# Block 1's recurrence in compact 64x64 tiles for all head pairs at once, its preparation inside the mixer's input product, attention scores from 64-row operands

## What is computed

```python
    for l in range(DEPTH):
        h = rms_norm(x, norm_ffn1[l])
        x = x + 0.5 * swiglu(h, ffn1_gate[l], ffn1_up[l], ffn1_down[l])
        h = rms_norm(x, norm_mix[l])
        p = h @ w_in[l]
...
    a = jax.nn.sigmoid(a0.astype(f32) + a_lo @ a2.astype(f32))
    g = jax.nn.sigmoid(g_lo) @ g2.astype(f32)
    kk = (k * k_k.astype(f32)).reshape(B, S, H, N)
    kk = kk / jnp.maximum(jnp.sqrt(jnp.sum(kk * kk, axis=-1, keepdims=True)), 1e-12)
...
    def step(state, inp):
        r_t, w_t, k_t, v_t, kk_t, b_t = inp
        sa = jnp.einsum('bhvk,bhk->bhv', state, -kk_t)
        state = (state * w_t[:, :, None, :] + sa[..., None] * b_t[:, :, None, :]
                 + v_t[..., None] * k_t[:, :, None, :])
        return state, jnp.einsum('bhvk,bhk->bhv', state, r_t)
```

## Time and profile before

| | |
|---|---|
| median of 3 runs | 3650.39 us (3649.76 to 3652.47) |
| the profiled execution | 3649.7 us, span 3647.9 us |
| instructions in the profile | 35779 |
| mean granted TensorE clock | 0.897 of full |

### The profile page before, as it was taken

One profiled execution on the slowest core, in us unless ns is written; L12 is line 12 of the kernel. 1 busy time (PEld: TensorE's weight loads), 2 busy tenths in 40 slices (PEclk: granted clock), 3 DMA queues, 4 the chain that ended last, 5 costly groups with the idle time before them and its releaser, 6 DMA issues. The chain is left out here.

```text
span 3647.9 us, 35779 instructions
## 1 busy us (share of the span) xinstructions
PE 3145.8 (86%) x14332; PEld 2549.1 (70%) x14332; DVE 1496.5 (41%) x1969; ACT 986.8 (27%) x1336; POOL 1204.2 (33%) x574
## 2 busy tenths in 40 slices
PE   8999978888699999999999998996534678999677
PEld 6888857778578888777887887884432556897346
DVE  4333435554443344745253221834676243000543
ACT  3222221110232232454233332112220142222131
POOL 3444432211134444553444443442000033444312
PEclk9999987777699999999999999997765689999878
DMA  3332210000023332222233233231210223332002
GB/s 129 97 102 96 87 61 1 1 0 1 1 87 96 93 105 92 81 81 81 93 98 93 93 98 109 88 98 47 15 21 19 41 85 96 93 93 93 0 18 75
DMA packets 91444, 251.28 MB, mean 69 GB/s; under 512 B 33440, under 2 KB 34592, under 8 KB 90400
## 3 DMA queue, kind: packets, MB, share of 16 engines
q1 hardware_dynamic: 82080, 247.09, 22.2%
q10 hardware_dynamic: 9216, 2.10, 0.3%
HBM read 240.51 MB, written 6.29 MB: 68 GB/s over the span
## 5 line engine op out<-in xcount | busy, mean ns | idle before, releaser
L436 POOL TENSOR_TENSOR weight_ring_r<-weight_ring,weight_hi_r 128x1024 fp32r<-128x1024 f32 (+2 forms) x412 | 1032.3, 2506 | 1641.6 <-ACT weight_hi_r L429 1641.6
L429 ACT ACTIVATE weight_hi_r<-weight_ring 128x1024 fp32r<-128x1024 f32 (+2 forms) x412 | 448.5, 1089 | 1637.1 <-PE acc L636 1275.1
L634 PE MATMUL acc<-p_r,weight_hi_r 128*128 128x512 f32 x1680 | 665.4, 396 | 19.1 <-POOL weight_ring_r L436 12.6
L636 PE MATMUL acc<-p_r,weight_ring_r 128*128 128x512 f32 x1680 | 659.6, 393 | 0.0
L635 PE MATMUL acc<-scr_r,weight_hi_r 128*128 128x512 f32 x1120 | 440.2, 393 | 0.0
L634 PEld LDWEIGHTS acc<-p_r,weight_hi_r 128*128 128x128 f32 x1680 | 316.4, 188 | 89.9 <-POOL weight_ring_r L436 19.4
L636 PEld LDWEIGHTS acc<-p_r,weight_ring_r 128*128 128x128 f32 x1680 | 316.3, 188 | 73.9
L635 PE MATMUL acc<-p_r,weight_hi_r 128*128 128x512 f32 x888 | 346.7, 390 | 0.0
L634 PE MATMUL acc<-scr_r,weight_hi_r 128*128 128x512 f32 x768 | 310.1, 404 | 15.6 <-DVE p_r L655 10.7
L636 PE MATMUL acc<-scr_r,weight_ring_r 128*128 128x512 f32 x768 | 304.9, 397 | 0.0
L635 PE MATMUL acc<-h_r,weight_hi_r 128*128 128x512 f32 x696 | 276.2, 397 | 0.0
(11 more groups left out here) (567 smaller groups left out, 4910.4 us busy)
## 6 DMA issues: line engine op xcount, KB each, us to landing
weight_ring<-in_weights SPq DMA_DIRECT2D x372, 512.0 KB, 3.5
weight_ring<-in_weights SPq DMA_DIRECT2D x32, 704.0 KB, 4.0
weight_ring<-in_weights SPq DMA_DIRECT2D x8, 640.0 KB, 3.9
x<-in_x SPq DMA_DIRECT2D x4, 512.0 KB, 6.9
lift<-h SPq DMA_DIRECT2D x1, 2048.0 KB, 8.8
p<-lift SPq DMA_DIRECT2D x8, 256.0 KB, 10.7
p<-lift SPq DMA_DIRECT2D x1, 2048.0 KB, 8.8
out<-x SPq DMA_DIRECT2D x1, 2048.0 KB, 6.3
```

Source lines behind the costliest of these rows:

```text
L429: self.nc.scalar.activation(self.r.weight_hi[:, ahead, 0:width], self.weight_ring[:, r, 0:width], ACT.Copy)\
L436: self.nc.gpsimd.tensor_tensor(rest, raw, hi, ALU.subtract).then_inc(self.weights_split, 1)
L634: pe.matmul(out, hi, op.hi(kx), start=kx == 0, stop=False)
L636: mm = pe.matmul(out, lo, op.hi(kx), start=False, stop=sub == g.q - 1 and k == g.kc - 1)
```

## The change

The recurrence runs once over all four pairs, on compact operands: each head keeps its 64 partitions, and a call takes 64 rows, 64 weight columns and 64 moving columns. `products` issues 32 calls for two pairs (two heads, eight chunks), neighbouring calls on different halves of the partitions and in different banks; `all_pairs` issues eight calls, one for each head. The masks shrink to 64 columns. `rwkv_lora_stage` is gone: the small products, the norms of the keys, the decays and the bonus are steps between the slots of the mix product on TensorE, ScalarE and GpSimd (the slots in `MIX_PE_AT`, `MIX_ACT_AT`, `MIX_POOL_AT`), and calls between the blocks on VectorE. `MIX_ORDER` brings the blocks in another order: first the gates' inputs, then k, r, v. The sums over a head go to `gather` and back by `spread` constants instead of `head_ones`. In attention, scores take their 64 rows of `p` directly, and GpSimd's copies and the zeroed `qz` are gone.

```diff
+    for pair in range(PAIRS):
+        head = 2 * pair + i // HEAD
+        parts.append((f"gather{pair}", (head[:, None] == i[None, :] % RW_HEADS).astype(np.float32)))
+        parts.append((f"spread{pair}", (i[:, None] == head[None, :]).astype(np.float32)))
...
+MIX_ORDER = (6, 2, 3, 0, 1, 4, 5, 7, 8, 9)
+MIX_PE_AT = (3, 4, 5, 6, 7, 8, 9, 11, 13, 15, 16)
+MIX_ACT_AT = (2, 3, 4, 5, 6, 7, 8, 9, 10, 11, 13)
+MIX_POOL_AT = (16, 17, 18)
+RW_R, RW_K, RW_V, RW_SIG, RW_A, RW_G, RW_B, RW_KP, RW_BON, RW_SUM, RW_E1 = 0, 4, 8, 20, 24, 28, 32, 36, 40, 44, 48
...
+            def side():
+                pe.wait_ge(core.consts_in, core.const_loads)
+                pe.wait_ge(q["lora_loaded"], 16)
+                pe.wait_ge(q["lo_act"], 1)
+                for i in range(PAIRS):
+                    if i:
+                        pe.wait_ge(q["sig"], i)
+                    at = slice(i * P, (i + 1) * P)
+                    mm(side_bank(0), lora[low, 0, at], p[low, LORA_W, :], start=True, stop=True)
+                    mm(side_bank(1), lora[high, 1, at], p[high, LORA_W, :], start=True, stop=True).then_inc(q["lora"], 1)
+                    yield
+                pe.wait_ge(q["sig"], PAIRS)
+                for i in range(PAIRS):
+                    if i >= 2:
+                        pe.wait_ge(q["g_read"], i - 1)
+                    mm(side_bank(i), lora[:, 2, i * P:(i + 1) * P], p[:, LORA_G, :], start=True, stop=True).then_inc(q["g_mm"], 1)
+                    if i % 2:
+                        yield
+                pe.wait_ge(q["g_read"], PAIRS)
+                for i in range(PAIRS):
+                    pe.wait_ge(q["k_sq"], i + 1)
+                    ins = mm(side_bank(0), C(f"gather{i}"), kp(i), start=(i == 0), stop=(i == PAIRS - 1))
+                ins.then_inc(q["k_sum"], 1)
+                yield
+                pe.wait_ge(q["k_root"], 1)
+                for i in range(PAIRS):
+                    if i >= 2:
+                        pe.wait_ge(q["k_read"], i - 1)
+                    mm(side_bank(i), C(f"spread{i}"), p[:, 50, :], start=True, stop=True).then_inc(q["k_back"], 1)
+                    if i % 2:
+                        yield
+                for i in range(PAIRS):
+                    pe.wait_ge(q["bonus_in"], i + 1)
+                    if i < 2:
+                        pe.wait_ge(q["k_read"], i + 3)
+                    else:
+                        pe.wait_ge(q["bonus_read"], i - 1)
+                    mm(side_bank(i), C("head_ones"), bon(i), start=True, stop=True).then_inc(q["bonus_sum"], 1)
+                    if i % 2:
+                        yield
+
+            steps = side()
...
+                    if product is mix and at in MIX_PE_AT:
+                        next(steps, None)
...
+            def exps(i):
+                act.wait_ge(q["cs"], i + 1)
+                if i >= 2:
+                    act.wait_ge(q["r_done"], i - 1)
+                a(e1(i), csum(i), ACT.Exp, scale=-DECAY_RATE)
+                a(sig(i), sig(i), ACT.Exp, scale=-DECAY_RATE).then_inc(q["exps"], 1)
+                act.wait_ge(q["exps"], 2 * i + 1)
+                a(csum(i), csum(i), ACT.Exp, scale=DECAY_RATE).then_inc(q["exps"], 1)
...
+            def rates(i):
+                dve.wait_ge(q["k_read"], i + 1)
+                dve.wait_ge(q["exps"], 2 * i + 2)
+                v.tensor_tensor(kk_(i), bb(i), sig(i), ALU.mult)
+                v.tensor_tensor(aa(i), bb(i), aa(i), ALU.mult).then_inc(q["rates"], 1)
...
+            read(0)
+            shift(0)
+            read(1)
+            shift(1)
+            raw_keys(0)
+            raw_keys(1)
...
+            def products(bank, d, left, right):
+
                 for j in range(2):
...
+                    for c in range(NLC):
+                        for i, row in ((2 * d, j), (2 * d + 1, 1 - j)):
+                            ins = mm(acc[head[row], bank + i % 2, at_c(c)], left(i)[head[row], at_c(c)], right(i, c)[head[row]],
+                                     start=True, stop=True)
+                return ins
+
+            at = lambda base: lambda i: p[:, base + i, :]
+            chunk = lambda f: lambda i, c: f(i)[:, at_c(c)]
+            ym1 = lambda i: scr[:, i, :]
+            identity = lambda i, c: eye
...
+            for d in range(2):
+                products(4 * d, d, at(RW_B), chunk(at(RW_K))).then_inc(q["a"], 1)
+                products(4 * d + 2, d, at(RW_K), chunk(at(RW_B))).then_inc(q["ts"], 1)
+            for n in range(N):
+                for d in range(2):
+                    pe.wait_ge(q["atn"], 2 * n + d + 1)
+                    if n == 0:
+                        pe.wait_ge(q["a_read"], 1)
+                        pe.wait_ge(q["tm_start"], d + 1)
+                    else:
+                        pe.wait_ge(q["tm"], 2 * (n - 1) + d + 1)
+                        pe.wait_ge(q["tt"], 2 * (n - 1) + 1)
+                    products(y_bank(n, d), d, at(RW_ATN), chunk(at(RW_TM))).then_inc(q["y"], 1)
+                for d in range(2):
+                    pe.wait_ge(q["y_read"], 2 * n + 1 + d)
+                    if n == 0:
+                        pe.wait_ge(q["a_read"], 2)
+                        pe.wait_ge(q["tt_start"], d + 1)
+                        pe.wait_ge(q["tm_start"], 2)
+                    else:
+                        pe.wait_ge(q["tt"], 2 * (n - 1) + 2)
+                        pe.wait_ge(q["tm"], 2 * (n - 1) + 2)
+                    if n < N - 1:
+                        products(z_bank(n, d), d, at(RW_TT), chunk(ym1)).then_inc(q["zm"], 1)
+                    products(z_bank(n, d) + 2, d, ym1, chunk(at(RW_TT))).then_inc(q["zt"], 1)
...
+            left = {"v": RW_V, "g": RW_KP, "f": RW_KP, "k": RW_KP, "e": RW_B, "b": RW_B}
+            right = {"g": RW_K, "f": RW_R, "e": RW_R}
+            free = {2: ("tt", 2 * N - 1), 3: ("tt", 2 * N), 4: ("unit_act", 1), 5: ("unit_act", 2), 6: ("unit_dve", 1), 7: ("unit_dve", 2),
+                    8: ("unit_dve", 3), 9: ("unit_dve", 4), 10: ("unit_act", 3), 11: ("unit_act", 4)}
+            for k, (name, d) in enumerate(UNIT):
+                if k in free:
+                    pe.wait_ge(q[free[k][0]], free[k][1])
+                products(UNIT_BANK[k % 4], d, at(left[name]), chunk(at(right[name])) if name in right else identity).then_inc(q["unit"], 1)
...
+            def all_pairs(out, left, right, start, stop):
+
+                for j in range(2):
+                    for i in (0, 2, 1, 3):
+                        row = j if i < 2 else 1 - j
+                        ins = mm(out(i)[head[row]], left(i)[head[row]], right(i)[head[row]], start=start(i), stop=stop(i))
+                return ins
...
+            all_pairs(w_of, of(RW_GT, 0), of(RW_V, 0), opens, closes).then_inc(q["w"], 1)
+            for c in range(NLC):
+                s_now = lambda i: of_pair(state[c % 2], i)
+                o_of = lambda i: acc[:, 4 + i, at_c(c)]
+                if c:
+                    pe.wait_ge(q["s_new"], c)
+                    all_pairs(w_of, of(RW_K, c), s_now, never, closes).then_inc(q["w"], 1)
+                    all_pairs(o_of, of(RW_R, c), s_now, every, never)
+                all_pairs(o_of, of(RW_FT, c), of(RW_V, c), lambda i: c == 0, never)
+                pe.wait_ge(q["w_read"], c + 1)
+                all_pairs(sa_of, of(RW_TT, c), lambda i: of_pair(w_now, i), opens, closes).then_inc(q["sa"], 1)
+                if c < NLC - 1:
+                    all_pairs(s_of, of(RW_KP, c), of(RW_V, c), opens, never)
+                    if c:
+                        all_pairs(s_of, lambda i: eye, s_now, never, never)
+                pe.wait_ge(q["sa_read"], c + 1)
+                if c < NLC - 1:
+                    all_pairs(s_of, of(RW_B, c), lambda i: of_pair(sa_now, i), never, closes).then_inc(q["s"], 1)
+                ins = all_pairs(o_of, of(RW_ET, c), lambda i: of_pair(sa_now, i), never, every)
+                if c < NLC - 1:
+                    all_pairs(w_of, of(RW_GT, c + 1), of(RW_V, c + 1), opens, never)
+            ins.then_inc(q["o"], 1)
+            for d in range(2):
+                pe.wait_ge(q["normed"], d + 1)
+                products(2 * d, d, at(RW_TM), identity).then_inc(q["turned"], 1)
...
+            for c in range(NLC):
+                dve.wait_ge(q["w"], c + 1)
+                v.tensor_copy(w_now.rearrange("p (a v) -> p a v", a=2), acc[:, 0:2, 0:P]).then_inc(q["w_read"], 1)
+                dve.wait_ge(q["sa"], c + 1)
+                v.tensor_copy(sa_now.rearrange("p (a v) -> p a v", a=2), acc[:, 0:2, P:2 * P]).then_inc(q["sa_read"], 1)
+                if c < NLC - 1:
+                    dve.wait_ge(q["s"], c + 1)
+                    v.tensor_tensor(four(state[(c + 1) % 2]), acc[:, 2:4, 0:P].rearrange("p a (b v) -> p a b v", b=2),
+                                    pend[:, :, :, c:c + 1].to_broadcast([P, 2, 2, HEAD]), ALU.mult).then_inc(q["s_new"], 1)
+            dve.wait_ge(q["o"], 1)
...
```

(41 more changed lines are left out.)

617 lines of the change are left out of this document (246 added, 371 removed).

## The result

The changed kernel takes **3401.0 us** (median of 4 executions, 3396.2 to 3404.0), the kernel before 3650.8 on the same chip; the ratio is 0.9314, 95% interval 0.9298 to 0.9330. The profiled execution took 3400.8 us with a span of 3399.0. That is 250 us less, where the forecast had 124 less and its range ended at 3430: the direction was right, the size wrong by a factor of two.

A forecast was written before the change was run, and what follows sets the result against it. TensorE was taken to bound the mix product, and the 64x64 call's price the new recurrence. Recurrence -161, mix product +30, attention -5, clock +12 gave -124 us: 3526 us, 8-in-10 range 3430 to 3700.

The forecast's parts named there:

- The price of a call: New recurrence on TensorE: a 64x64 call with 64 moving columns costs 0.12 us, 1936 calls 232 us; bounds 0.056 and 0.22.
- the first rival: 64x64 calls of the recurrence: neighbouring calls overlap, price 0.06 to 0.08 us, 97 us less, 3430 us; chance 0.13.
- The other price rules: Trainium skill's rules for a 64x64 call: two weight loads 0.107 us, or two matmuls at the issue gap 0.124 us.
- Waits: TensorE in the new recurrence: 4 us, at the start, between operands and chunks, and in the last chunk.
- just enough: Chunks: 16 calls cover each VectorE round trip of about 0.9 us; at 0.056 us a call the cover is 0.9.
- The norm, the barrier, the handover: Ends of the new recurrence: norm for all pairs 23 us, barrier after the mix product 1.6, handover to attention 0.6.
- The mix product: Gets 30 us longer: 24 added TensorE calls of 512 columns, 20.5 us, and 10 us of stalls.
- The second rival: Mix product: VectorE falls behind, TensorE waits 30 us or more, more chunks at lower clock; 3560 to 3630 us; chance 0.13.
- Attention: Score groups with two halves of the partitions side by side, copies gone: 5 us of gain, between 0 and 8.
- The clock: New recurrence: one TensorE call in sixteen runs at the lower clock, 12 us of cost.
- The third rival: Whole `rwkv_stage`: TensorE's clock falls to 1.2 GHz and stays there, 0.22 us a call, 3714 us; chance 0.13.
- The fourth rival: Recurrence calls: each costs 0.22 us whatever its shape, at full clock, 3726 us; chance 0.10.

The follow-up runs named there:

- the probe of four quadrants: Changed kernel with extra 128-call stretches ahead of the chunks; in this one 64x64 calls take all four quadrants in turn: 0.048 us a call by distance of starts.
- the serial stretch: Changed kernel with extra 128-call stretches ahead of the chunks; in this one 64 calls on one half, then 64 on the other: 0.116 us a call.
- the run without the carry: Changed kernel without the eight identity calls a chunk that carry the state on (part of the computation left out): 3394.4 us in one execution.
- the edit alone: Kernel before with only attention's part of the change: 3650.7 us against 3652.6 us, ratio 0.9993.
- the order by halves: Changed kernel with each group of 16 (or 4) 64x64 calls on one half before the other's: 3474.3 us in one execution, 3591.0 to 3592.5 in three.

## Why the prediction was wrong

**The price of a call: the step that failed.** "Both say 0.11, ... I take 0.12". Alone it is 0.116, so both estimates were right for a call by itself; but the forecast put the overlap of neighbouring calls at nothing, and with it the price is 0.0583, near the lower bound of 0.056. 1936 x (0.12 - 0.0583) = 119 us, nearly all of the 125 by which the forecast missed. This was the first rival, and it had 0.13. What I put against it was a misreading: that the fastest records of the earlier trace rows take 0.22 shows what a load of 128 weight columns costs, and says nothing of how fast instructions can be issued; the probe of four quadrants starts a call every 0.029 us while it runs. That the two records of one call share a half is true and changes nothing: the overlap is with the next call. The fact that the code alternates halves call by call was known, and `products` was the larger part. The Trainium skill, "TensorEngine Tiling (Array Packing)", says in Key Properties that different tiles load weights and multiply in parallel, and in Theoretical Speedup that a dimension of 64 gives up to twice the speed. The probe agrees: 0.116 against 0.058.

**The other price rules.** The Trainium skill, "TensorE: Matmul & The Clock Gate", LDWEIGHTS (loading the stationary operand), takes a load as its columns over 1.2 GHz. For two loads of 64 columns that is an estimate of 0.107 us a call; the serial stretch's 0.116 agrees within a tenth. Its Back-to-back issue gap has about 62 ns a matmul where the sequencer decodes them itself, at least 0.124 us a call; alternating calls, two matmuls each, take 0.058, so that case is not met here.

**Waits.** 4 us were forecast, 6.1 measured; the largest is the mask of the second half, 4.5, at the start, where I said the cover is missing. That the cover in the chunks would be "just enough" at 0.056 came true: the run without the carry shows 0.18 us to spare.

**The norm, the barrier, the handover.** 19.4, 1.7 and 0.4 us, forecast 23, 1.6 and 0.6.

**The mix product.** 30 us were forecast, 28.4 measured. A slot's 24 instructions take 24 x 0.231 = 5.54 us, so a gate step costs 6.81 - 5.54 = 1.27; 4 of them and 16 calls x 0.86 are 18.8, where the forecast had 20.5. The wait is 6.4. Another 2.7 lie behind it at a clock of 0.50: the same instructions take 507.89 - 502.01 = 5.88 us there and 515.23 - 512.08 = 3.15 at the next step. The last 0.5 are not placed. The wait stands in the bonus step, but for `k_read` (L1397), not `bonus_in`; VectorE is busy 92.7 us, as forecast above 90. The calls of `k_back` did not wait. The second rival, stalls of 30 us or more, did not come about.

**Attention.** 5 us were forecast; the edit alone gives 4.6 in the trace of attention, and nothing that the whole time shows. The changed kernel has 8.1.

**The clock.** 12 us were forecast as cost. The clock is 0.92 to 1.00 in the new stage up to the norm, 0.62 in it; what of its 145.7 us the other terms leave is 145.7 - 112.9 - 6.1 - 1.7 - 19.4 - 0.4 = 5 us. The third rival did not come about here; three executions of the order by halves had its clock, 0.50 in the inversion, and were 191 us longer.

**The fourth rival**, a fixed price, is refuted by 0.116 for one half against 0.224 for 128x128 at full clock.

**What was luck.** The other errors nearly cancel. Clock, norm, product, attention and barrier with handover came out 15 us better than forecast, the waits 2 worse, and 8 us ahead of the product and behind attention had no term; together 5 of the 125.

## What to carry to other kernels

Where small matmuls have a choice of order, let neighbours differ in the half of the input or of the output partitions: here that halved their price, and a reordering of loops into groups of 16 cost 73 us in one execution and, with the clock at half, 191 in three. A record's duration (218 ns here) is not its price (0.058 us a call); take the price from the distance of starts, look for a pause inside that distance, and do not read an issue limit out of a row in which something else is the bound. And an edit's lower price may use up the cover of the round trips beside it, so work out the cover at both ends of the price.

## What the hardware showed that was not expected

- Rows different or columns different is enough for two calls to overlap: 0.058 us with the output half fixed, 0.059 with the input half fixed, 0.116 with both fixed.
- Four quadrants in turn cost 0.029 us a call, a quarter of 0.116, while they run; after 116 calls came a pause of 1.9 us with no cause in the profile, which makes it 0.048 over the stretch. Whether a kernel can keep that pace is not shown.
- With the halves alternating, 32 moving columns cost as much as 64 (0.058), 128 at full clock 0.109.
- TensorE busy without a gap is not enough for full clock: one half only, 512 calls, stood at 0.50; and 128x128 by 64 columns ran for 43 us at 1.00 in one probe and for 54 us near 0.50 in the other.
